# A second half of an out-projection taken four runs at a time for both token tiles, a weight unit released at the end of its first half, and small retention work moved to Pool

## Chip, cores and metric

The kernel runs on one core of a Trainium2 chip. The metric is device time in microseconds; the program is one launch. Three runs of the kernel before gave 1143.90, 1144.95 and 1144.04 us, median 1144.04 us.

## What is computed

A decoder of two layers over 256 tokens of width 1024, in float32. Cut to what matters:

```python
for layer in range(2):
    mixer = even_mixer if layer == 0 else odd_mixer      # MoBA (8 heads) + retention (4 heads) | 16 dilated heads
    h = h + mixer(rms_norm(h, mix_norm), w_in, w_out)    # ends in  concat(heads) @ w_out   (1024 x 1024)
    h = h + hier_moe(rms_norm(h, ffn_norm), ...)         # router: best of 4 groups, best 2 of its 8 experts
out = rms_norm(h, final_norm)

# retention: y = (scores * decay) @ v;  r_out = (y - mean) * rsqrt(var + eps) * silu(rg)
# expert:    y_e = (silu(x @ w_gate[e]) * (x @ w_up[e])) @ w_down[e]
```

With 256 tokens the mixers see two tiles of 128 tokens. Every one of the 32 experts of each layer is loaded and computed, with 32 slots an expert in a round.

## The kernel before

**Memory.** Weights stream through a ring of 12 units of 2 MB. In the expert loop units 0 to 7 hold four pairs (gate and up), units 8 to 11 four down matrices. Before the expert loop of a layer units 0 to 5 hold the input projection, units 6, 7, 8 and 11 activations, and `W_OUT_AT = (9, 10)` the two halves (512 output columns each) of the out-projection. `load_first` on SP issues the first four pairs and downs in a fixed order: pairs as the projection frees their units, then down 0 after the last values product, then downs 2 and 3 after the last product of the out-projection (`mixed` at 2T), then down 1, into unit 9, after the last logits. After that each load waits until the product that reads its unit is done (`next_pair`, `next_down`). SP's queue is in order.

**Precision.** The two projections are made of three fp32r products each: high by high, low by high, high by low. ACT makes the high part of a weight chunk (a copy to fp32r), DVE the low part (a subtraction). For the out-projection this is `split_mix` on ACT and `low_mix` on DVE, chunk by chunk in the order `MIX_TURNS`. A chunk is `(n, i)`: half n, run i of eight along the inner dimension. The low part overwrites the weight in place, the high part goes to one of three buffers of `mix_parts` (in `scratch`), to `mix_first` (four, in `xn`), or, for half 1 and i from 4 on, to `mix_last`, which lies in unit 9. `MIX_WAITS` holds how many uses of parts must be past before a buffer is written again.

**Out-projection (PE).** The first half is made for both tiles run by run (`mix_both`), in part between the last heads. Then PE's order is written out by hand: of the second half tile 0's runs 0 to 2, the turn (four transposes) of tile 0's first half, runs 3 and 4, the turn of tile 1's first half, runs 5 to 7; then tile 1's runs 0 and 1, turn, logits, runs 2 and 3, two blocks of logits, runs 4 to 7, and last tile 1's turn and logits. DVE adds each finished bank to h (`add_mixed`, L1589), ACT squares it for the norm and copies the turned parts to `hT`; tile 1's lie in unit 9.

**Routing.** `route` on DVE, once per tile, makes from the logits the best group, the best two experts and the one-hot sum `asg` (L1392 to L1416); PE sums places (L1199 to L1205) with a filler product (`keep_warm`, L879) between the two tiles; DVE makes the slot matrix (L1442); PE gathers the tokens (L990, 32 matmuls) and runs the first gate and up (L1008). Tile 0's normed rows are scaled on DVE (`scale_rows`, L1260), tile 1's on ACT (L834).

**Attention of layer 0.** PE makes scores (L938, L941) and transposes (L966), DVE mask and maximum (L1332), ACT the exponentials (L664), DVE reciprocals of the sums (L1345, L1346), Pool scales the probabilities (L622), ACT copies the turned ones (L672). Retention's group norm lies between the heads on DVE (`retention_step`): statistics, from Pool a power (L617), at m = 5 a Newton step of four operations (L1373 to L1376), at m = 6 and 7 the norm (L1382) and the product with the gate (L1385). The gate is made earlier by `swish`, in four pieces of 256 columns of three DVE operations each (L1284 add, L1285 reciprocal, L1286 product), two of them in the projection.

## Time and profile before

| what | value |
|---|---|
| three runs | 1143.90, 1144.95, 1144.04 us |
| profiled execution, its own time | 1143.11 us |
| its span | 1141.2 us |
| PE busy, share of the span | 863.9 us, 76% |
| DVE busy | 392.7 us, 34% |
| ACT busy | 239.8 us, 21% |
| POOL busy | 29.1 us, 3% |
| HBM read, mean rate | 439.01 MB, 386 GB/s |
| chain that ended last | PE 42%, DMA 39%, SPq 5%, DVE 5% |

The shares are averages over stages. The span falls into an input projection and attention of layer 0 (to about 103 us), its out-projection and routing (to 142), its expert loop (to 568), and the same for layer 1 (attention to 663, out-projection and routing to 701, experts to the end). In rows of the timeline a row is start, duration, engine, line, operation, operands and count, and in brackets the idle time before it and what ended it. Durations of neighbouring matmuls overlap, so their starts tell the pace.

### The profile page before, as it was taken

To read this page: it belongs to the slowest core of one execution; us is meant where nothing else is said; L and a number is where in the kernel's file an instruction comes from. 1 tells how busy PE (TensorE), PEld (TensorE's weight loads), DVE (VectorE), ACT (ScalarE), POOL (GpSimd) and SP (SyncE) were. 2 spreads that over 40 slices of the span, in tenths; PEclk is the share of its full clock that TensorE was granted. 3 is DMA by queue.
4 is the path that set the end of the run, shared out by engine and by line. 5 is a ranking of instruction groups with operands and counts; after the bars stand their busy time and mean duration, and the time that the engine had idled before them with its cause. 6 is when DMAs were issued, how large, how long until landed. Compare 5 with 4: busy or idle time off the path is not lost.

```text
span 1141.2 us, 21777 instructions
## 1 busy us (share of the span) xinstructions
PE 863.9 (76%) x9146; PEld 549.3 (48%) x9146; DVE 392.7 (34%) x988; ACT 239.8 (21%) x622; POOL 29.1 (3%) x47
## 2 busy tenths in 40 slices
PE   8999879976575757576799998798566666666774
PEld 6876745534243424243478776355243434343432
DVE  6887623322021212121188764233121212121212
ACT  5554401110010000000165762011000000000012
POOL 0002000000000000000000210000000000000000
PEclk9997979988787878788999998899787879797887
DMA  9866699999999999999997576999999999999995
GB/s 350 275 285 265 270 396 422 427 430 428 428 430 427 430 428 427 430 429 427 415 386 293 213 296 239 418 426 429 428 428 430 426 430 429 428 429 428 428 429 215
DMA packets 54417, 440.70 MB, mean 386 GB/s; under 512 B 11874, under 2 KB 12386, under 8 KB 29539
## 3 DMA queue, kind: packets, MB, share of 16 engines
q1 hardware_dynamic: 54368, 440.07, 92.9%
q8 instruction: 30, 0.49, 0.2%
q14 instruction: 17, 0.13, 0.0%
q10 hardware_dynamic: 2, 0.00, 0.0%
HBM read 439.01 MB, written 1.05 MB: 386 GB/s over the span
## 4 chain that ended last, share of the span: by engine, by line
PE 42%; DMA 39%; SPq 5%; DVE 5%; another core or an unknown queue 3%; ACT 3%; issue 2%; POOLq 0%; POOL 0%; ACTq 0%; DVEq 0%
DMA ring<-in_w_expert_up 21%; DMA ring<-in_w_expert_down 17%; PE bank L1008 12%; PE bank L1029 5%; PE bank L902 3%; PE bank L904 3%; PE bank L903 3%; PE bank L990 3%; SPq L441 3%; PE bank L1042 3%; PE bank L1090 1%; SPq L445 1%; PE bank L1092 1%; PE bank L1091 1%
## 5 line engine op out<-in xcount | busy, mean ns | idle before, releaser
L1008 PE MATMUL bank<-ring,scratch 128*32 128x256 f32 x4096 | 300.5, 458 | 176.9 <-DMA ring<-in_w_expert_up 175.5
L1008 PEld LDWEIGHTS bank<-ring,scratch 128*32 128x32 f32 x4096 | 155.1, 131 | 317.8 <-issue 207.0
L1471 DVE TENSOR_SCALAR scratch<-scratch 128x128 f32<-128x128 f32 x64 | 14.6, 227 | 632.2 <-ACT scratch L698 610.4
L697 ACT ACTIVATE scratch<-bank 128x128 f32<-128x128 f32 x64 | 17.8, 278 | 589.4 <-PE bank L1008 570.7
L1029 PE MATMUL bank<-ring,h 128*32 128x256 f32 x2048 | 127.4, 390 | 12.6 <-DMA ring<-in_w_expert_down 12.4
L1042 PE MATMUL bank<-h 32*128 32x256 f32 x1024 | 75.2, 407 | 37.2 <-ACT h L705 37.2
L1029 PEld LDWEIGHTS bank<-ring,h 128*32 128x32 f32 x2048 | 63.2, 111 | 57.3 <-issue 25.1
L1042 PEld LDWEIGHTS bank<-h 32*128 32x128 f32 x1024 | 50.6, 188 | 67.1 <-issue 67.0
L902 PE MATMUL bank<-split,h_high 128*128 128x512 f32 x192 | 77.2, 402 | 4.3 <-DVE split L1276 3.7
L904 PE MATMUL bank<-split,h_high 128*128 128x512 f32 x192 | 75.0, 391 | 0.0
L903 PE MATMUL bank<-split,h_low 128*128 128x512 f32 x192 | 74.9, 390 | 0.0
L1276 DVE SCALAR_TENSOR_TENSOR split<-ring,gains,split 128x512 fp32r<-128x512 f32 x96 | 67.9, 748 | 17.5 <-ACT split L744 16.8
L744 ACT ACTIVATE split<-ring,gains 128x512 fp32r<-128x512 f32 x96 | 65.5, 722 | 22.6 <-PE bank L904 20.9
L990 PE MATMUL bank<-scratch,xn 128*128 128x128 f32 x512 | 64.9, 288 | 1.7 <-DVE scratch L1442 1.7
L990 PEld LDWEIGHTS bank<-scratch,xn 128*128 128x128 f32 x512 | 61.9, 201 | 7.7 <-issue 7.7
L1472 DVE RECIPROCAL scratch<-scratch 128x128 f32<-128x128 f32 x64 | 61.0, 953 | 2.2
L705 ACT COPY h<-bank 128x256 f32<-128x256 f32 x64 | 23.8, 372 | 108.0 <-PE bank L1029 108.0
L1020 PE MATMUL bank<-cst,h 128*128 128x128 f32 x128 | 28.5, 305 | 21.5 <-DVE scratch L1459 11.0
L902 PEld LDWEIGHTS bank<-split,h_high 128*128 128x128 f32 x192 | 36.1, 188 | 14.1 <-DVE split L1276 6.7
L703 ACT COPY h<-bank 128x256 f32<-128x256 f32 x64 | 24.6, 385 | 72.4 <-PE bank L1020 72.2
L904 PEld LDWEIGHTS bank<-split,h_high 128*128 128x128 f32 x192 | 36.0, 188 | 7.9
L903 PEld LDWEIGHTS bank<-split,h_low 128*128 128x128 f32 x192 | 36.1, 188 | 6.9
(181 smaller groups left out, 742.8 us busy)
## 6 DMA issues: line engine op xcount, KB each, us to landing
ring<-in_w_expert_gate SPq DMA_DIRECT2D x64, 2048.0 KB, 47.3
ring<-in_w_expert_up SPq DMA_DIRECT2D x64, 2048.0 KB, 48.8
ring<-in_w_expert_down SPq DMA_DIRECT2D x62, 2048.0 KB, 48.4
ring<-in_w_in_even SPq DMA_DIRECT2D x5, 2048.0 KB, 17.5
ring<-in_w_in_odd SPq DMA_DIRECT2D x5, 2048.0 KB, 20.6
ring<-in_w_out_even SPq DMA_DIRECT2D x2, 2048.0 KB, 8.9
ring<-in_w_expert_down SPq DMA_DIRECT2D x4, 1024.0 KB, 44.6
ring<-in_w_out_odd SPq DMA_DIRECT2D x2, 2048.0 KB, 12.9
```

Of the source, the lines that this page charges most:

```text
L441: sp.dma_start(ring[:, unit, :], gate_rows[row]).then_inc(pair_arrived[l][k], 16)
L744: act.activation(w_high[u % PARTS], ring[:, j, 512 * c:512 * c + 512], ACT.Copy, scale=gains[:, 2 * l, c:c + 1]).then_inc(w_high_ready, 1)
L902: pe.matmul(bank, high, wh, start=(c == 0), stop=False)
L903: pe.matmul(bank, low, wh, start=False, stop=False)
L904: last = pe.matmul(bank, high, wl, start=False, stop=(c == C - 1))
L990: last = pe.matmul(psum[4 + c // 4][:, P * (c % 4):P * (c % 4) + P], xn_c[:, t, c, :], onehot[:, t, :, :].rearrange("p k s -> p (k s)"), s ...
L1008: last = pe.matmul(psum[6][32 * j:32 * j + 32, 0:2 * P].rearrange("p (a s) -> p a s", a=2), xT[:, c, SLOTS * k:SLOTS * k + SLOTS], ring[:, ...
L1020: last = pe.transpose(psum[7][:, P * t:P * t + P], gated[k][:, t, :, :].rearrange("p b s -> p (b s)"), ident)
L1029: last = pe.matmul(psum[4][32 * q:32 * q + 32, 0:QUARTER], hidT[k][:, 32 * j:32 * j + 32], ring[:, DOWN_AT[k], D * j + QUARTER * q:D * j + ...
L1042: last = pe.matmul(acc[q][:, t, :], gatedT[rows, P * t:P * t + P], y_sb[rows, :], start=False, stop=last_expert and t == T - 1, tile_posit ...
L1276: dve.scalar_tensor_tensor(out=w_low[u % PARTS], in0=ring[:, j, 512 * c:512 * c + 512], scalar=gains[:, 2 * l, c:c + 1], in1=w_high[u % PA ...
L1472: chain.link(dve.reciprocal(eb, eb))
```

## The change

Six things are altered. (1) PE's order in the second half of the out-projection: runs 4 to 7 for both tiles first, then the turns and the rest. (2) Where the high parts of the weights go: none lies in unit 9 any more, nor do tile 1's turned rows nor the squares' unused output; the counted waits follow. (3) SP loads down 1 after the first half (`mixed` at T). (4) Routing on DVE: tile 1's add before tile 0's routing, fewer operations, side results last; both tiles' rows are scaled on ACT. (5) Filler products on PE: two for one, and one of 256 columns before the gather. (6) On Pool: swish's add and product (512 columns at once), retention's Newton step, and the product of the normed rows with the gate; and one reciprocal for a head in place of two. Several semaphores of two layers become one, counted on.

```diff
-MIX_PART = (0, 1, 2, 3, 0, 1, 2, 0)
-MIX_WAITS = {(0, 4): 1, (0, 5): 2, (0, 6): 3, (0, 7): 5, (1, 3): 4}
-MIX_PARTS = 5
+MIX_PART = {(0, 0): 0, (0, 1): 1, (0, 2): 2, (0, 4): 0, (0, 5): 1, (0, 6): 2, (0, 7): 0,
+            (1, 4): 1, (1, 5): 2, (1, 6): 0, (1, 7): 1}
+MIX_WAITS = {(0, 4): 1, (0, 5): 2, (0, 6): 3, (0, 7): 5, (1, 3): 4, (1, 4): 6, (1, 5): 7, (1, 7): 8}
+MIX_PARTS = 8
+MIX_FIRST, MIX_LAST = (0, 4), (C - 1, 3)
-MIX_TURNS = (..., (0, 6), (1, 0), (0, 7), (1, 1), (1, 2), (1, 3), (1, 4), (1, 5), (1, 6), (1, 7))
+MIX_TURNS = (..., (0, 6), (1, 0), (0, 7), (1, 1), (1, 2), (1, 4), (1, 5), (1, 6), (1, 7), (1, 3))
...
@@ load_first (SP)
                 load_down(l, l * EXPERTS, 0)
+                sp.wait_ge(mixed, 2 * T * l + T)
+                load_down(l, l * EXPERTS + 1, 1)
                 sp.wait_ge(mixed, 2 * T * l + T * 2)
                 for k in range(2, GE):
                     load_down(l, l * EXPERTS + k, k)
-                sp.wait_ge(logits_done, T * (l + 1))
-                load_down(l, l * EXPERTS + 1, 1)
@@ gpsimd
+                if l == 0:
+                    for t in range(T):
+                        pool.wait_ge(bank_out[0][(RG * T + t) % 4], RG * T // 4 + 1)
+                        pool.tensor_tensor(rg[:, t, :], rg[:, t, :], const("ones")[:, 0:1].broadcast_to([P, 512]),
+                                           ALU.add).then_inc(swish_begun, 1)
+                        pool.wait_ge(swish_turned, T * (t + 1))
+                        pool.tensor_tensor(rg[:, t, :], rg[:, t, :], o_ret[:, t, :], ALU.mult).then_inc(swished, 1)
                 for m in range(HEADS[l]):
                     if l == 0 and m == 3:
                         pool.wait_ge(ret_var, 1)
+                        steps = ((rrstd, rvar, wide(half_exp[:, 0:1]), ALU.pow), (newton, rrstd, rrstd, ALU.mult),
+                                 (newton, newton, rvar, ALU.mult), (newton, newton, wide(half_exp[:, 0:1]), ALU.mult),
+                                 (newton, newton, wide(three_halves), ALU.add), (rrstd, rrstd, newton, ALU.mult))
+                        for n, (o, a, b, op) in enumerate(steps):
+                            pool.tensor_tensor(o, a, b, op).then_inc(ret_pow, 1)
+                            pool.wait_ge(ret_pow, n + 1)
...
+                    if l == 0 and m >= HEADS[0] - T:
+                        t = m - (HEADS[0] - T)
+                        pool.wait_ge(ret_scaled, t + 1)
+                        pool.wait_ge(swished, t + 1)
+                        pool.tensor_tensor(o_ret[:, t, :], o_ret[:, t, :], rg[:, t, :], ALU.mult).then_inc(ret_normed, 1)
@@ scalar
                 for t in range(T):
                     if t:
-                        act.wait_ge(rstd_ready, T * (2 * l + 1) + t + 1)
                         act.wait_ge(logits_done, T * l + t + 1)
-                        act.activation(xn_c[:, t, :, :], ...).then_inc(xn_scaled, 1)
+                    else:
+                        act.wait_ge(mix_xn_used, l + 1)
+                    act.wait_ge(rstd_ready, T * (2 * l + 1) + t + 1)
+                    act.activation(xn_c[:, t, :, :], h_c[:, t, :, :], ACT.Copy,
+                                   scale=rstd[:, t:t + 1]).then_inc(xn_scaled, 1)
+                for t in range(T):
                     act.wait_ge(gmax_ready, T * l + t + 1)
@@ tensor
-                mix_product(l, 1, 0, order[:3])
+                for i in order[4:]:
+                    for t in range(T):
+                        mix_product(l, 1, t, (i,))
                 turn_mixed(l, 0, 0)
-                mix_product(l, 1, 0, order[3:5])
+                mix_product(l, 1, 0, order[:2])
                 turn_mixed(l, 1, 0)
-                mix_product(l, 1, 0, order[5:])
+                mix_product(l, 1, 0, order[2:4])
                 pe.wait_ge(w_rt_ready, 1)
                 mix_product(l, 1, 1, order[:2])
                 turn_mixed(l, 0, 1)
                 logits(l, 0, 0)
                 mix_product(l, 1, 1, order[2:4])
                 logits(l, 0, 1)
+                turn_mixed(l, 1, 1)
                 logits(l, 1, 0)
-                mix_product(l, 1, 1, order[4:])
-                turn_mixed(l, 1, 1)
                 logits(l, 1, 1)
...
-                keep_warm(1, cst[:, 0:512], psum[0])
+                keep_warm(2, cst[:, 0:512], psum[0])
                 pe.wait_ge(assigned, T * l + 2)
...
-                pe.wait_ge(xn_ready, l + 1)
-                pe.wait_ge(xn_scaled, l + 1)
+                keep_warm(1, cst[:, 0:256], psum[0])
+                pe.wait_ge(xn_scaled, T * (l + 1))
@@ vector
-            def scale_rows(l, t):
...
             def swish(t, half, link):
-                link(dve.tensor_scalar(e, e, 1.0, None, ALU.add))
-                link(dve.reciprocal(e, e))
-                link(dve.tensor_tensor(e, e, gate_in, ALU.mult))
+                dve.wait_ge(swish_begun, t + 1)
+                dve.reciprocal(e, e).then_inc(swish_turned, 1)
...
-                dve.reciprocal(rden[:, m, 0:2], den[:, m, :])
-                dve.reciprocal(rden[:, m, 2:3], den[:, m, 1:2]).then_inc(den_ready[l], 1)
+                dve.reciprocal(rden[:, m % RDENS, :, :], den[:, m, :].unsqueeze(2).broadcast_to([P, T, 2])).then_inc(den_ready, 1)
...
                 elif m in (6, 7):
+                    if t == 0:
+                        dve.wait_ge(ret_pow, 6)
+                        dve.wait_ge(swished, T)
...
-                    dve.tensor_tensor(o_ret[:, t, :], o_ret[:, t, :], rg[:, t, :], ALU.mult).then_inc(ret_normed, 1)
...
                 if l == 0:
+                    swish(1, 0, link)
                     for n in range(2, RET):
                         decayed(n)
-                    swish(1, 0, link)
+                    swish(1, 1, link)
...
                 for t in range(T):
+                    low_mix(*late[t])
                     add_mixed(0, t)
-                    low_mix(*late[t])
...
-                for t in range(T):
-                    add_mixed(1, t)
-                    variance(2 * l + 1, t, 3 + t)
-                    inverse_root(2 * l + 1, t)
-                    if t == 0:
-                        scale_rows(l, t)
-                    route(l, t, route_link)
+                add_mixed(1, 0)
+                variance(2 * l + 1, 0, 3)
+                inverse_root(2 * l + 1, 0)
+                add_mixed(1, 1)
+                route(l, 0, route_link, lambda: variance(2 * l + 1, 1, 4))
+                inverse_root(2 * l + 1, 1)
+                route(l, 1, route_link)
```

In `route` the two casts of indices to float are gone (the comparisons read the integer indices), the penalty's factor is folded into one operation with the add, and the negated maximum and the difference of the best two (L1397, L1408) come after the one-hot sum.

## Rows read from the trace of the kernel before

**Rows 1.** Windows, core 0: length, busy us (x) of PE PEld DVE ACT POOL, clock, DMA, GB/s.

```profile
126.00:128.00 2.00, 2.00 (x17) 1.79 (x15) 0.68 (x3) 1.23 (x3) 0.41 (x1) 1.00 0.02 8
142.00:144.00 2.00, 1.99 (x9) 2.00 (x10) 0.85 (x6) 0.00 (x0) 1.12 (x4) 0.51 0.99 426
150.00:152.00 2.00, 1.28 (x25) 0.54 (x21) 0.00 (x0) 0.54 (x2) 0.00 (x0) 1.00 0.32 131
300.00:560.00 260.00, 172.59 (x2157) 98.55 (x2161) 50.43 (x117) 20.98 (x69) 0.00 (x0) 0.84 1.01 428
```

**Rows 2.** Waits of the DMA issuing queue: queue, line, releaser, total us, times, longest.

```profile
SPq L445 <- PE bank L1092: 40.7, 2, 20.4
```

**Rows 3.** Chain that ended last, layer 0, out-projection's end: start, us, work.

```profile
134.31 0.70 DVE h L1589
...
136.38 1.09 PE bank L1128 x8
142.01 5.43 PE bank L990 x32
147.44 3.63 PE bank L1008 x64
...
183.13 3.78 PE bank L990 x32
```

**Rows 4.** The same chain, layer 1.

```profile
694.63 1.62 PE bank L1128 x8
697.52 1.87 PE bank L879 x2
701.22 5.72 PE bank L990 x32
```

**Rows 5.** Timeline of PE, second half of the out-projection, layer 0.

```profile
119.11 0.39 PE L1090 MATMUL bank<-mix_first,o_high 128*128 128x512 f32 x1
...
129.57 0.98 PE L1128 MATMUL bank<-w_rt,scratch 128*128 128x36 f32 x8
...
131.27 0.48 PE L1090 MATMUL bank<-mix_last,o_high 128*128 128x512 f32 x1
...
133.88 0.39 PE L1092 MATMUL bank<-mix_low,o_high 128*128 128x512 f32 x1
...
137.97 1.10 PE L879 MATMUL bank<-cst 128*128 128x512 f32 x2
```

**Rows 6.** Timeline of DVE, routing of the second token tile, layer 0.

```profile
140.26 0.19 DVE L1416 TENSOR_TENSOR asg<-scratch 128x32 f32<-128x32 f32 x1
```

**Rows 7.** Timeline of ACT, the scaling of xn for tile 1, layer 0.

```profile
137.56 2.14 ACT L834 ACTIVATE xn<-h,small 128x1024 f32<-128x1024 f32 x1 [0.85 <-PE bank L1128]
```

**Rows 8.** Timeline of DVE, attention of layer 0.

```profile
93.99 0.75 DVE L1373 TENSOR_TENSOR small<-small 128x8 f32<-128x8 f32 x1
...
95.77 0.17 DVE L1376 TENSOR_TENSOR small<-small 128x8 f32<-128x8 f32 x1
```

**Rows 9.** Timeline of POOL, attention of layer 0.

```profile
92.28 1.65 POOL L617 TENSOR_TENSOR small<-small 128x8 f32<-128x8 f32 x1 [0.58 <-DVE small L1368]
93.89 1.61 POOL L622 TENSOR_TENSOR ring<-ring,small 128x384 f32<-128x384 f32 x2
```

**Rows 10.** Timeline of POOL, gate weights, layer 0.

```profile
142.62 0.20 POOL L605 TENSOR_TENSOR small<-small 128x2 f32<-128x2 f32 x1
```

**Rows 11.** Waits of PE in 84 to 104 us: line, releaser, total us, times, longest.

```profile
PE bank L938 <- DVE small L1332: 1.5, 2, 0.9
PE bank L966 <- ACT xn L672: 0.6, 1, 0.6
```

**Rows 12.** Timeline of PE, projection of layer 0, its one stall.

```profile
67.07 0.50 PE L902 MATMUL bank<-split,h_high 128*128 128x512 f32 x1 [0.89 <-DVE split L1276]
```

**Rows 13.** Chain that ended last, one head of layer 1.

```profile
656.25 0.14 DVE small L1346
```

More of the change, by code:

```diff
@@ L66 @@
 PROBS = 6
+RDENS = 12
 EXPERTS = 32
@@ L277, in build, with hT @@
         xT = scratch[:, 0:1024].rearrange("p (c s) -> p c s", c=C)
-        hT = [xT, ring[:, W_OUT_AT[0], 2048:2048 + D].rearrange("p (c s) -> p c s", c=C)]
+        hT_late = [v.rearrange("p (c s) -> p c s", c=C // 2) for v in (scratch[:, 1024:1536], xn[:, 1024:1536])]
+        def hT(t, q):
+            return hT_late[q] if t else xT[:, 4 * q:4 * q + 4, :]
         onehot = scratch[:, 1024:1280].rearrange("p (t k s) -> p t k s", t=T, k=GE)
@@ L303, in build @@
         top = small[:, 152:184].rearrange("p (a e) -> p a e", a=2 * T)
-        idx = small[:, 184:190]
         gv = small[:, 192:208]
@@ L314, in build @@
         cnt = small[:, 316:318]
+        three_halves = small[:, 318:319]
+        newton = small[:, 258:266]
         posm = sb("posm", [P, T, 36])
@@ L634, in square @@
                 if ph % 2:
-                    unused = mix_bank(1, t)[:, :] if half else ring[:, W_OUT_AT[0], 3072 + 512 * t:3584 + 512 * t]
+                    unused = mix_bank(1, t)[:, :] if half else psum[4 + t][:, :]
                 else:
@@ L665, in exponentials @@
                                           accum_out=den[:, m, t:t + 1])
-                last.then_inc(exp_done[l], 1)
+                last.then_inc(exp_done, 1)
             def copy_pT(l, m):
@@ L687, in split_mix @@
                     act.wait_ge(pair_done[l], HEADS[l] // 2)
-                if n and i == C // 2:
+                if (n, i) == (1, 6):
                     act.wait_ge(mixed, 2 * T * l + T)
@@ L878, in keep_warm @@
                 for _ in range(n):
-                    pe.matmul(bank[:, :], data[:, 0:P], data, start=True, stop=True)
+                    pe.matmul(bank[:, 0:data.shape[1]], data[:, 0:P], data, start=True, stop=True)
             def turn_part(ph, t, q):
@@ L1089, in mix_product @@
                     out = mix_bank(n, t)[:, :]
-                    pe.matmul(out, high, mix_high(n, i), start=(i == 0), stop=False)
+                    pe.matmul(out, high, mix_high(n, i), start=(i == MIX_FIRST[n]), stop=False)
                     pe.matmul(out, low, mix_high(n, i), start=False, stop=False)
-                    last = pe.matmul(out, high, mix_low[n][:, c, :], start=False, stop=(i == C - 1))
-                    if (n, t) == (0, 1) and i < MIX_PARTS:
+                    last = pe.matmul(out, high, mix_low[n][:, c, :], start=False, stop=(i == MIX_LAST[n]))
+                    if t and (i < C - 1 if n == 0 else i == MIX_FIRST[1]):
                         last.then_inc(mix_part_used, 1)
@@ L1127, in logits @@
                 for c in range(4 * q, 4 * q + 4):
-                    last = pe.matmul(psum[4 + t][:, 0:36], hT[t][:, c, :],
+                    last = pe.matmul(psum[4 + t][:, 0:36], hT(t, q)[:, c - 4 * q, :],
                                      w_rt[:, l, c, :], start=(c == 0), stop=(c == C - 1))
@@ L1383, in retention_step, with route @@
                                                  rstat[:, t, n, 0:1], rrstd[:, at:at + 1], ALU.subtract, ALU.mult)
-                    link(last)
-                    dve.tensor_tensor(o_ret[:, t, :], o_ret[:, t, :], rg[:, t, :], ALU.mult).then_inc(ret_normed, 1)
-            def route(l, t, link):
+                    last.then_inc(ret_scaled, 1)
+            def route(l, t, link, between=None):
                 dve.wait_ge(logits_done, T * l + t + 1)
@@ L1406, in route @@
                 best = top[:, T + t, :]
                 link(dve.max(best, masked[:, t, :]))
+                if between:
+                    between()
+                link(dve.max_index(idx_u[:, T + t, :], best, masked[:, t, :]))
+                link(dve.tensor_tensor(chosen[:, t, :, :],
+                                       const("iota")[:, 0:EXPERTS].unsqueeze(1).broadcast_to([P, 2, EXPERTS]),
+                                       idx_u[:, T + t, 0:2].unsqueeze(2).broadcast_to([P, 2, EXPERTS]), ALU.is_equal))
@@ L1408, in route @@
+                dve.tensor_tensor(asg[:, t, :], chosen[:, t, 0, :], chosen[:, t, 1, :], ALU.add)\
+                   .then_inc(assigned, 1)
+                dve.tensor_scalar(gv[:, t:t + 1], top[:, t, 0:1], -1.0, None, ALU.mult)
                 dve.tensor_tensor(gv[:, 6 + t:7 + t], best[:, 1:2], best[:, 0:1], ALU.subtract)\
                    .then_inc(gmax_ready, 1)
-                link(dve.max_index(idx_u[:, T + t, :], best, masked[:, t, :]))
-                pair = idx[:, 2 + 2 * t:4 + 2 * t]
@@ L1555, in _ @@
                         head_max(l, m)
-                    if l == 0 and m == 1:
-                        swish(1, 1, link)
                     if l == 0 and m == HEADS[l] + 2:
```

89 lines of the change are left out of this document (35 added, 54 removed).

## The prediction

> **What bounds the kernel now.** First the windows. From 300 to 560 us, inside the first layer's expert loop, the DMA engines are busy for the whole stretch (share 1.01) and move 428 GB/s [rows 1]: there the time is bytes over rate, and no engine's speed counts. In front of each expert loop it is different. At 126 to 128 us the share is 0.02, because the ring is full or the next unit is not yet given up, and at 150 to 152 us it is 0.32 [rows 1]. The issuing queue stood up to 20.4 us before the loads of the second half's weight units, for the out-projection's last product [rows 2]. But those loads are done by about 150.6 us, and the next one can be issued only when the first expert's gate-up matmuls, which begin at 147.44 and last 3.63 us, have given up their pair [rows 3]: 151.1 us. So the end of that first gate-up decides, once per layer: all later bytes of the layer follow it, and each us that it comes earlier is a us of the kernel. Third, the chain: in front of it lie the residual add at 134.31, the last logits at 136.38, the gather at 142.01, the gate-up at 147.44 [rows 3], and in layer 1 the same steps [rows 4].
>
> **The tail of the out-projection, reordered.** One product is three matmuls; the last four run from 131.27 to 134.1, where the matmul of 133.88 hands over [rows 5], so one takes some 0.7 us, or 0.68 with the handover at its start taken off. The second half has 16 of them and begins at 119.11. Before, two blocks of logits (129.57 to 131.27, 1.70 us [rows 5]) and the first tile's products stand ahead of the last four products, which end at 133.88 + 0.39 = 134.3. After, eight products for both tiles come first, then three turns of some 0.4 us, four products for each tile and one block of logits between: the last product ends at 119.1 + 16 x 0.68 + 1.2 + 0.8 + 0.2 = 132.3, about 2.0 us earlier. The price is that tile 0 is complete only at 128.2. Its norm takes some 3 us, to 131.5, and its logits end at 133.2, which is when DVE turns to its routing. So tile 0's routing, which was hidden under tile 1's products, now runs while tile 1's last logits are made, and DVE becomes the one that is late: routing 0 from 133.2, with tile 1's variance between, to 136.2, two short steps of the root to 136.8, routing 1 to its one-hot sum at 139.1. That sum stood at 140.26 + 0.19 = 140.45 [rows 6], so of the 2.0 us 1.35 arrive. Counted in this is that the two casts go (an estimate of 0.2 us each, from the 0.19 us of the small operation beside them [rows 6]) and that the two side results move behind the sum. The scaling of xn goes to ACT for both tiles, 2.14 us each (137.56 [rows 7]): it begins after the last turned copy, at 134.5, and ends near 139.0, and DVE's scaling goes. It stays under the routing, 1.6 us before the gather; if that cover went it would cost what it overruns. The new parts buffers wait on products that are at least 1 us past when their copy is due, so I cost these waits at nothing. SP's load for expert 1 moves from behind the logits to the end of the first half: that empties the queue earlier, but the first gate-up's end still decides, so 0.
>
> **The clock.** The gather of 32 matmuls takes 3.78 us at full clock (183.13 [rows 3]), but 5.43 at 142.01 [rows 3] and 5.72 at 701.22 [rows 4]; the granted clock is 0.51 at 142 to 144 us [rows 1], that is 1.2 GHz, after a stretch in which PE had only turns, logits and waits. The change puts two filler products of 512 columns where one was, and a short one just before the gather. Three outcomes, counted from the second half's start. (a) The rate never falls: gather from 140.65 to 144.4, against 147.44: 3.0 us saved; layer 1, whose part runs at half rate from the logits on (1.62 against 1.09 us), saves 4.3: 7.3 together. (b) It falls in the thin stretch, which has grown longer, since the products that stood behind the logits now stand before them. The fillers then hold PE: one took 1.10 us at full [rows 5] and 1.87 at half [rows 4], so two are 3.7, and they end 2.2 us after the sum that they were to bridge; but the rate is back for the gather: 0.6 and 1.8 saved, 2.4 together. (c) It falls later and the gather is slow as well: 1.2 lost together. I take 2.9, near (b) with a part of (a), because already the shorter stretch of before lost the rate in layer 1.
>
> **Attention of layer 0.** DVE is the bound at its start: scores wait 1.5 us in two waits for DVE's masks, and a transpose 0.6 us for a copy that is late for the same reason [rows 11]. The change takes from DVE the swish adds and products, the Newton steps (one of them takes 0.75 us [rows 8]) and the two 512-column products. The matmuls run at half rate in that stretch and are nearly gapless from 92 us, so no more than those 2.1 us can be won, and not less than 0: I take 1.1 (0.5 at the start, 0.6 at the copy). Pool's part: its power of 8 columns takes 1.65 us [rows 9], a product of 2 columns 0.20 [rows 10]; the five steps are products and sums, so 0.28 us each with the wait (an estimate): 1.4 us, behind which the fourth head's scaling queues. It is then ready at 95.9, and PE wants it at 96.7. The last two products of 512 columns (1.07 us each, from 0.80 for 384 [rows 9]) end near 101.4, and PE wants them at 104.
>
> **Projection of layer 0.** PE has one stall, 0.89 us, behind the swish on DVE [rows 12]. Without its adds and products 0.3 us of it would go. But the two engines get in each other's way: a DVE product of 8 columns with two operands from SBUF took 0.75 us while Pool worked (93.99 [rows 8] inside 93.89 to 95.50 [rows 9]) and 0.17 after (95.77 [rows 8]). Pool's four passes of 1.07 us now lie among the splits of the weights, which are such operations. With no collision 0.3 is won; with every pass in the way 4.3 - 0.3 = 4.0 is lost. I take 0.6 lost, two passes of which half is covered by the four split buffers. The Trainium skill (GPSIMD Engine Reference, Key points) says that Pool shares its SBUF interfaces with VectorE and collides with operations of two SBUF inputs, and that elementwise work is about twice as fast on DVE; by that rule alone the move to Pool gains nothing. The trace agrees on the collision.
>
> **Layer 1's attention.** One reciprocal in place of two for each head: the second one is 0.14 us in the chain [rows 13], some 0.09 after overlap, in about 6 of 16 heads: 0.5 us.
>
> **Sum**, against the profiled execution (1143.11 us, span 1141.2): -2.9 - 1.1 + 0.6 - 0.5 = -3.9, so 1139.2. The three runs shown (1143.9 to 1144.95) are 0.8 to 1.8 above that execution, whose gathers were not at their slowest; I keep 1139.2 for the after kernel's median, since its tail price is a middle one already.
>
> **Rivals.** R1: the first gate-up's end is not what decides, the transfers are: then nothing moves, 1143.1. For it: 428 GB/s for most of the time. Against it: share 0.32 and 0.02 just in front [rows 1]. It also stands for gains eaten up by collisions of 2 to 4 us. R2: outcome (a) in both layers, 1143.1 - 7.3 - 1.0 = 1134.8. For it: the filler is doubled. Against it: the thin stretch grows. R3, slower: Pool's Newton steps cost as its power of the same width does, 1.65 us [rows 9] and not 0.28. Five of them hold the fourth head until 103, against PE's 97.0 of before; PE, in order, loses 5.9 us in place of winning 1.1, and the sum is 1143.1 + 5.9 - 2.4 - 0.5 + 0.1 = 1146.2, with the tail as in (b) and 0.1 lost in the projection. It decides above 0.45 us a step. Against it: 0.20 for two columns [rows 10]. R4: the change doesn't do as it says: a late buffer (the last parts copy waits on a product of the same half) stalls PE inside the eight products; each us of that takes one us of the tail, so up to the 1.35 in each layer: 1141.9.
>
> **How the numbers follow.** Forecast 0.60, R1 0.13, R2 0.12, R3 0.06, R4 0.09. A measurement of this kernel tells 0.2 per cent, 2.3 us, from no change, so the bounds are 1141.8 and 1146.3. Faster: forecast's part below 1141.8 (0.54), R2 0.12, half of R4 and a part of R1: 0.76. Slower: half of R3 and twice-failed cases, 0.06. Same: 0.18. Extremes of the terms are 1132 (all best) and 1146.5; the range leaves out R3 and half of R2: 1135.3 to 1143.4.
>
> **What would show it.** Right: last product of the second half 13.2 us after its start in both layers, the sum of the second routing 1.3 us earlier, gathers at 3.8 us, the first gate-up's end 2 to 4 us earlier in each layer after taking off what attention gave, DMA share near 1 from there. In layer 0 the mix begins 0.5 us earlier, DVE's splits of 0.75 us are longer beside Pool. Wrong: the DMA share below 1 behind the first gate-up; PE stalls inside the eight products; Pool's steps above 0.45 us; fillers at 1.9 us and a slow gather together.

## The result, and the profile after

Four runs of the changed kernel gave 1134.06 to 1136.33 us, median 1135.59; four of the kernel before, interleaved with them, 1143.90 to 1146.07, median 1144.49. The ratio is 0.9919, interval 0.9903 to 0.9935: 8.9 us faster. The forecast was 1139.2, from 1135.3 to 1143.4: the sign was right, the time lies just inside the low end of the range, and the gain is more than twice the 3.9 us of the sum. The profiled execution took 1135.6 us (span 1133.7), 7.5 us less than the one of before.

Page of the changed kernel: busy time, rates, and the chain's shares.

```profile
PE 861.8 (76%) x9154; PEld 547.3 (48%) x9154; DVE 383.3 (34%) x940; ACT 244.2 (22%) x624; POOL 37.8 (3%) x59
HBM read 439.01 MB, written 1.05 MB: 388 GB/s over the span
PE 43%; DMA 40%; SPq 5%; DVE 4%; another core or an unknown queue 3%; ACT 3%; issue 2%; POOL 0%; POOLq 0%; ACTq 0%; DVEq 0%
```

PE's work is the same. DVE has 9.4 us less, Pool 8.7 us more, and neither number is near the 7.5 us or has to be: what counts is when each layer's first gate-up ends. Windows of the changed kernel, columns as in [rows 1]:

```profile
126.00:128.00 2.00, 2.00 (x15) 1.72 (x13) 1.00 (x3) 0.91 (x3) 0.10 (x1) 1.00 0.88 377
142.00:144.00 2.00, 2.00 (x32) 1.45 (x35) 0.69 (x1) 0.00 (x0) 0.00 (x0) 1.00 0.02 8
300.00:560.00 260.00, 172.29 (x2164) 98.60 (x2168) 49.75 (x116) 21.41 (x71) 0.00 (x0) 0.84 1.01 428
```

The expert loop is what it was (share 1.01, 428 GB/s). The DMA engines now work at 126 us, where they stood at 0.02, because the load into unit 9 goes out after the first half; and they stand still at 142 to 144, until the gate-up is done. The chain of the changed kernel, out-projection's end to gate-up, layer 0 (start, us, work):

```profile
134.36 3.22 PE bank L910 x4
137.58 0.27 PE bank L1236 x2
...
139.07 3.81 PE bank L1021 x32
142.88 3.63 PE bank L1039 x64
```

and layer 1:

```profile
694.44 0.41 PE bank L1236 x2
...
695.94 3.81 PE bank L1021 x32
699.75 3.63 PE bank L1039 x64
```

Beside [rows 3] and [rows 4]: the gather takes 3.81 us in both layers, where it took 5.43 and 5.72, and the gate-up begins 4.6 us earlier in layer 0 and some 7.2 us earlier in layer 1 (699.75 against 706.94).

The span splits into these stages, from the timelines (us). Each runs from the first matmul of one kind to the first of the next; attention begins with the last projection product. Before and after are one profile each:

| stage | before | after | gain |
|---|---|---|---|
| start, to the first projection product | 9.77 | 10.65 | -0.9 |
| projection, layer 0 | 72.56 | 72.11 | 0.45 |
| attention, layer 0, to the first out-projection product | 20.77 | 18.63 | 2.1 |
| out-projection, first half, layer 0 | 16.01 | 15.33 | 0.7 |
| **tail, layer 0**: second half's first product to first gate-up | 28.26 | 26.10 | 2.2 |
| expert loop, layer 0 | 425.85 | 427.49 | -1.6 |
| projection, layer 1 | 70.31 | 70.31 | 0 |
| attention, layer 1 | 20.03 | 20.26 | -0.2 |
| out-projection, first half, layer 1 | 13.79 | 13.79 | 0 |
| **tail, layer 1** | 29.52 | 25.01 | 4.5 |
| the rest | 434.32 | 434.07 | 0.25 |

The start and the expert loops vary by about 1 us between kernels that don't differ there (9.1 to 10.7, and 425.9 to 427.5 in the profiles below), so the two losses are nothing to explain. The two tails are 6.7 us, attention and the first half 2.8. The name "second sum" below is for the one-hot sum of tile 1's routing, the last step of DVE that PE's place sums wait for.

### The profile page after: what moved, and what is told of

It is laid out like the page before. It is cut to its first block, busy times and chain, and to the rows that moved or that the text cites. A ratio compares the mean times of both kernels' runs of the same rounds, so it can differ in the third digit from the quotient of the medians.

```text
span 1133.7 us, 21763 instructions
## 1 busy us (share of the span) xinstructions
PE 861.8 (76%) x9154; PEld 547.3 (48%) x9154; DVE 383.3 (34%) x940; ACT 244.2 (22%) x624; POOL 37.8 (3%) x59
## 4 chain that ended last, share of the span: by engine, by line
PE 43%; DMA 40%; SPq 5%; DVE 4%; another core or an unknown queue 3%; ACT 3%; issue 2%; POOL 0%; POOLq 0%; ACTq 0%; DVEq 0%
DMA ring<-in_w_expert_up 30%; PE bank L1039 13%; DMA ring<-in_w_expert_down 9%; PE bank L1060 5%; PE bank L933 3%; PE bank L935 3%; PE bank L934 3%; SPq L449 3%; PE bank L1073 3%; PE bank L1021 2%; PE bank L1121 1%; SPq L453 1%; PE bank L1123 1%; PE bank L1122 1%
## 5 line engine op out<-in xcount | busy, mean ns | idle before, releaser
L1060 PEld LDWEIGHTS bank<-ring,h 128*32 128x32 f32 x2048 | 63.1, 111 | 55.8 <-issue 24.1
L772 ACT ACTIVATE split<-ring,gains 128x512 fp32r<-128x512 f32 x96 | 65.5, 722 | 21.7 <-PE bank L935 20.3
L1021 PE MATMUL bank<-scratch,xn 128*128 128x128 f32 x512 | 61.4, 278 | 0.7 <-DVE scratch L1459 0.7
L1021 PEld LDWEIGHTS bank<-scratch,xn 128*128 128x128 f32 x512 | 58.4, 192 | 7.2 <-issue 7.2
```

The lines of the kernel that those rows point to most:

```text
L772: act.activation(w_high[u % PARTS], ring[:, j, 512 * c:512 * c + 512], ACT.Copy, scale=gains[:, 2 * l, c:c + 1]).then_inc(w_high_ready, 1)
L1021: last = pe.matmul(psum[4 + c // 4][:, P * (c % 4):P * (c % 4) + P], xn_c[:, t, c, :], onehot[:, t, :, :].rearrange("p k s -> p (k s)"), s ...
L1060: last = pe.matmul(psum[4][32 * q:32 * q + 32, 0:QUARTER], hidT[k][:, 32 * j:32 * j + 32], ring[:, DOWN_AT[k], D * j + QUARTER * q:D * j + ...
```

## Experiments

Twelve kernels were run, each timed in five rounds beside the kernel before (1143.86, 1144.78 and 1144.2 us median in the three groups of four). Lengths named "tail" are those of the table.

| kernel | median us | ratio to before, interval | tail 0 | tail 1 |
|---|---|---|---|---|
| the changed kernel again | 1135.39 | 0.9920 (0.9905 to 0.9936) | 26.1 | 26.1 |
| Pool's moves undone | 1137.52 | 0.9945 (0.9930 to 0.9960) | 25.0 | 26.1 |
| one filler | 1139.72 | 0.9960 (0.9944 to 0.9976) | 26.6 | 27.8 |
| kernel before with the fillers | 1142.82 | 0.9985 (0.9975 to 0.9995) | 26.6 | 27.5 |
| down 1 loaded late | 1137.83 | 0.9934 (0.9917 to 0.9952) | 25.0 | 25.0 |
| tile 1's add late | 1145.53 | 1.0008 (0.9999 to 1.0017) | 31.8 | 31.2 |
| two reciprocals | 1134.14 | 0.9909 (0.9895 to 0.9923) | 25.0 | 27.2 |
| Newton step on DVE | 1134.90 | 0.9915 (0.9900 to 0.9930) | 25.8 | 25.9 |
| swish and gate products on DVE | 1135.41 | 0.9928 (0.9913 to 0.9944) | 25.0 | 25.0 |
| tile 1's add late, one filler | 1146.30 | 1.0026 (1.0016 to 1.0035) | 30.8 | 32.1 |
| long fillers of 384 columns | 1134.45 | 0.9918 (0.9903 to 0.9933) | 25.0 | 25.0 |
| one more short filler | **1133.63** | 0.9914 (0.9900 to 0.9928) | 25.0 | 25.0 |

**The changed kernel again**, unaltered, for the spread.

> The changed kernel once more, to see how its gain falls on the stages when the clock's falls lie elsewhere. Every theory: 1134 to 1137 us. Order theory (the reordered products and the shorter routing bring the one-hot sum earlier): the second routing's sum ends 19.7 us after the second half's start in both layers, as in the profile seen, against 21.3 and 21.9 before. Clock theory (most of the tail's gain is that the gather runs at full rate): the gather takes 3.8 us in both layers again, and in neither layer the way from second half to first gate-up is longer than 27 us (28.3 and 29.5 before).

1135.39 us, the same. The second sum ended 19.7 us after the second half's start in both layers, and the gather took 3.81 us in both, as either theory had it. Its layer 1 tail was 26.1 where the first profile had 25.0, so a tail alone varies by 1.1 us; the next section comes back to it.

**All of Pool's new work back on DVE**, the merged reciprocal kept.

```diff
-                        pool.tensor_tensor(rg[:, t, :], rg[:, t, :], o_ret[:, t, :], ALU.mult).then_inc(swished, 1)
...
+                link(dve.tensor_scalar(e, e, 1.0, None, ALU.add))
+                link(dve.reciprocal(e, e))
+                link(dve.tensor_tensor(e, e, gate_in, ALU.mult))
...
-                        for n, (o, a, b, op) in enumerate(steps):
+                    link(dve.tensor_tensor(step, rrstd, rrstd, ALU.mult))
...
-                        pool.tensor_tensor(o_ret[:, t, :], o_ret[:, t, :], rg[:, t, :], ALU.mult).then_inc(ret_normed, 1)
+                    dve.tensor_tensor(o_ret[:, t, :], o_ret[:, t, :], rg[:, t, :], ALU.mult).then_inc(ret_normed, 1)
```

> The changed kernel with swish, Newton step and the gate's product back on DVE. If the move to Pool is what made attention of layer 0 shorter (20.8 us before, 18.6 after from last projection product to first mix product), it takes 20.5 to 21 us again and the kernel is 2 to 3 us slower than the changed one, 1137.6 to 1138.6. Rival: attention is shorter because the clock fell 2.8 us later in it; then it stays at 18.6 to 19.3 and the kernel is within 0.5 us of the changed one.

1137.52, between the two expectations, so the moves are worth 2.1 us. The projection is 72.55 (72.11 with the moves) and attention 19.79 (18.63): 1.6 of them lie there, and PE's time at half rate in attention was 6.8 us in both profiles. The waits of PE in its attention of layer 0 (line, releaser, total, times, longest), first here and then in the changed kernel:

```profile
PE bank L951 <- DVE small L1340: 2.2, 3, 0.9
PE bank L979 <- ACT xn L682: 1.1, 1, 1.1
```

```profile
PE bank L969 <- DVE small L1356: 2.0, 3, 0.7
PE bank L997 <- ACT xn L700: 0.4, 1, 0.4
```

The moves shorten one wait for a late copy (1.1 to 0.4) and hardly the waits for masks. The kernel before had 1.5 and 0.6 [rows 11], no more than the changed kernel's 2.0 and 0.4: from before to after, PE's waits in this stretch did not shrink.

**One filler**: the changed kernel with the filler products of before.

```diff
-                keep_warm(2, cst[:, 0:512], psum[0])
+                keep_warm(1, cst[:, 0:512], psum[0])
...
-                keep_warm(1, cst[:, 0:256], psum[0])
```

> The changed kernel with one filler product of 512 columns, as before, and without the short one. Clock theory: the gather runs at half rate in at least one layer (5.4 us and more), the kernel is 2 to 4 us slower than the changed one, 1137.6 to 1139.6. Order theory: the fillers only fill; within 0.7 us of the changed one, and where the rate has fallen PE reaches the second routing's sum up to 1 us earlier.

1139.72: 4.3 us slower than with them, as the clock theory had it. Timeline of PE in this kernel, layer 0:

```profile
134.15 1.10 PE L910 MATMUL bank<-cst 128*128 128x512 f32 x2
136.43 0.41 PE L1236 MATMUL bank<-asg,cst 128*128 128x32 f32 x2 [1.18 <-DVE asg L1429]
...
137.93 5.44 PE L1021 MATMUL bank<-scratch,xn 128*128 128x128 f32 x32 [0.87 <-DVE scratch L1458]
```

PE idles 1.18 us behind its filler and 0.87 before the gather, the granted clock is 0.63 at 138 to 140 us, and the gather takes 5.44 us (6.25 in layer 1).

**The kernel before with the fillers**, nothing else changed but that a filler writes only as many columns as it reads.

```diff
-                keep_warm(1, cst[:, 0:512], psum[0])
+                keep_warm(2, cst[:, 0:512], psum[0])
...
+                keep_warm(1, cst[:, 0:256], psum[0])
                 pe.wait_ge(xn_ready, l + 1)
```

> The kernel before with two filler products of 512 columns and the short one, nothing else. Clock theory: most of the tail's 6.6 us of gain come from them, 3 to 5 us faster than before, 1139.5 to 1141.5. Order theory: the stretch from last product to second sum is long enough already and the gather's rate differs by chance; 0 to 1.5 us faster, 1143 to 1144.5.

1142.82, 1.0 us faster in the median (1.7 by the ratio), although its tails are 1.6 and 2.0 us shorter in the profile. The gather ran at full rate in both layers, 3.81 us, as the clock theory had it, but the 3 to 5 us that it gave did not come. Its projection was 1.25 us longer in the profile, 73.81: the granted clock was 0.50 from 12 to 15 us, among the first projection products. The kernel with two reciprocals (73.4) has the same, and in the one with the Newton step on DVE (73.0) matmuls ran at half pace up to 13.8 us. So, in one profile each, fillers alone shorten the two tails by 3.7 us, the new order and routing alone (the kernel with one filler) by 3.4, and both together by 5.6 to 7.8; in the median, fillers alone are worth 1.0 to 1.7 us.

**Down 1 loaded late**, behind the last logits as before.

```diff
-                sp.wait_ge(mixed, 2 * T * l + T)
-                load_down(l, l * EXPERTS + 1, 1)
...
+                sp.wait_ge(logits_done, T * (l + 1))
+                load_down(l, l * EXPERTS + 1, 1)
```

> The changed kernel with expert 1's down matrix loaded after the last logits again, as before. Theory that the first gate-up's end decides: nothing, within 0.7 us of the changed kernel; the three loads begun at the last product are done 12.9 + 14.7 us after the second half's start, 1.6 us behind the first gate-up's start and before its end. Rival, the transfers decide now that the gate-up comes earlier: 1 to 4 us slower than the changed kernel.

1137.83, 6.9 us under its kernel before where the changed kernel has 8.5: 1.5 us less gain, though the intervals overlap. Both tails are 25.0, so it is not PE. A window of this kernel, and the same one of the changed kernel:

```profile
700.00:705.00 5.00, 4.28 (x80) 2.35 (x76) 0.00 (x0) 0.54 (x2) 0.00 (x0) 1.00 0.92 354
```

```profile
700.00:705.00 5.00, 4.28 (x84) 2.34 (x80) 0.47 (x1) 0.54 (x2) 0.00 (x0) 1.00 0.22 49
```

The next pair was issued at 702.6 here, but the DMA engines were still busy with the downs (0.92 against 0.22): the pair stands behind them. The rest of layer 1 took 436.6 us, against 433.4 to 434.9 in all other profiles. In layer 0 the expert loop took 427.0, inside the spread of the others, so the loss shows in one layer alone.

**Tile 1's add and variance behind tile 0's routing**, as DVE had them before.

```diff
                 inverse_root(2 * l + 1, 0)
-                add_mixed(1, 1)
-                route(l, 0, route_link, lambda: variance(2 * l + 1, 1, 4))
+                route(l, 0, route_link)
+                add_mixed(1, 1)
+                variance(2 * l + 1, 1, 4)
```

> The changed kernel with tile 1's add and variance behind tile 0's routing, as before. The add would come 2.3 us after its product instead of at once, and with it the last turn and logits: second sum at about 22 us after the second half's start instead of 19.7, kernel 2 to 4 us slower than the changed one. Rival, clock: the fillers hide it, since after a fall PE is late anyway; under 1 us slower.

1145.53: 0.75 us above its kernel before, where the changed kernel is 8.5 below: a loss of 9 us, far above what either theory expected. Its timeline of PE, layer 0:

```profile
133.69 1.00 PE L916 MATMUL bank<-cst,h 128*128 128x128 f32 x4 [3.19 <-DVE h L1605]
...
139.03 3.76 PE L910 MATMUL bank<-cst 128*128 128x512 f32 x4
142.58 0.47 PE L1236 MATMUL bank<-asg,cst 128*128 128x32 f32 x2
```

and of DVE:

```profile
140.15 0.19 DVE L1430 TENSOR_TENSOR asg<-scratch 128x32 f32<-128x32 f32 x1
```

Tile 1's last product was done at 129.7, but DVE routed tile 0 until 132.9, so PE stood 3.19 us. In the kernel before the two fell together: there the last product ended at 134.3 and the routing sum had been done since 133.5. The turn and the logits behind the wait then ran at half rate (the granted clock was low from 133.9 for 10.2 us), and so did the fillers, 3.76 us, so that PE came to the sum, ready at 140.34, only at 142.58. Tail 31.8 against 26.1: 4.3 of the 5.7 us lie in the second sum, which comes 24.0 us after the second half's start and not 19.7, and 1.3 in the fillers.

**The same with one filler.**

> The changed kernel with tile 1's add and variance behind tile 0's routing, and with the one filler of the kernel before in place of two and a short one: the new order of products with both other helpers of the tail taken away. With the fillers there, the late add cost 10 us (1145.5), 4.3 us a tail of it in the second sum and the rest in fillers that ran at half rate and ended 2.4 us behind that sum. Theory A (the add is what the new order needs, the fillers only add to its price): the second sum stays at 24.0 us after the second half's start, PE is free when it comes, but the gather is at half rate: tails of 31.0 to 32, median within 1.5 us of 1145.5. Theory B (the 10 us are mostly the fillers'): tails of 28.5 to 29.5 us as in the kernel before, median 1140 to 1142.

1146.3, tails 30.8 and 32.1: as the theory that the add is the cause had it, but for layer 0's second sum, which came at 23.0 us and not 24.0 (24.1 in layer 1). Layer 0:

```profile
137.61 2.06 PE L910 MATMUL bank<-cst 128*128 128x512 f32 x2
139.46 0.47 PE L1236 MATMUL bank<-asg,cst 128*128 128x32 f32 x2
...
141.22 5.55 PE L1021 MATMUL bank<-scratch,xn 128*128 128x128 f32 x32 [0.87 <-DVE scratch L1458]
```

What the shorter filler gives back (0.5 us behind the sum in place of 2.2), the gather takes (5.55 for 3.81). The change without the early add and the fillers is 2.1 us slower than the kernel before.

**Two reciprocals per head.**

```diff
-                dve.reciprocal(rden[:, m % RDENS, :, :], den[:, m, :].unsqueeze(2).broadcast_to([P, T, 2])).then_inc(den_ready, 1)
+                for t in range(T):
+                    last = dve.reciprocal(rden[:, m % RDENS, t, :], den[:, m, t:t + 1].broadcast_to([P, 2]))
+                last.then_inc(den_ready, 1)
```

> The changed kernel with two reciprocals for each head again. My forecast's term: 0.5 us slower, all in layer 1's attention (20.3 us to 20.8 from last projection product to first mix product). Rival, the profile seen: layer 1's attention took 20.03 us before and 20.26 and 20.27 after, so the single reciprocal brings nothing; within 0.3 us in that stretch.

1134.14, not slower: layer 1's attention is 20.04 us with two reciprocals, and 19.9 to 20.3 in the profiles with one. No gain of the merged operation can be told.

**Newton step back on DVE.**

> The changed kernel with the Newton step alone back on DVE. Attention of layer 0 took 18.6 us in the changed kernel and 19.8 with all of the small work back on DVE. If the Newton step makes that difference (its products collide with Pool's scaling, 0.75 us each), 19.6 to 20.2 and 1 to 1.5 us slower; if the swish and gate products make it, 18.6 to 18.9 and within 0.4 us.

1134.90, no difference that can be told. Attention took 19.34 us, which fits neither expectation, but PE ran at half rate for 10.2 us of it and not for 6.8 (next section). On Pool the step was six operations in 3.05 us:

```profile
92.41 3.05 POOL L639 TENSOR_TENSOR small<-small 128x8 f32<-128x8 f32 x6 [0.58 <-DVE small L1391]
```

so 1.4 us more than the power alone [rows 9], 0.28 a step. By the time, it does not matter which engine does it.

**Swish's adds and products and the gate products back on DVE**, the Newton step left on Pool.

> The changed kernel with the gate's adds and products (swish) and the product of the normed rows with the gate back on DVE; retention's Newton step stays on Pool. Theory A (these large operations, and not the Newton step, are what attention and the projection's stall gained): projection 72.5 us (72.1 in the changed kernel), last projection product to first out-projection product 19.8 us (18.6), median 1.5 to 2.2 us above the changed kernel's, as with all moves to Pool undone (1137.5). Theory B (the Newton step carries half of it): 19.2 us, median at most 1 us higher.

1135.41, ratio 0.9928: between the two theories. The projection is 72.60. The 0.89 us stall of [rows 12] stands in all four profiles with swish on DVE and in none of the ten with it on Pool, so the 0.5 us there are these operations'. Attention is 19.54, and it was 19.34 with the Newton step back; kernels with every move had 19.3 to 19.6 where the low stretch of the clock was as long as in these two, 10.2 us (next section). So each group alone costs attention nothing there. Both together cost 1.1 us, but that pair of profiles had a low stretch of 6.8 us; no profile has both moves undone at 10.2 us, or one of them at 6.8. Whether the moves pay only together, or only where the low stretch is short, stays open.

**Long fillers of 384 columns.**

```diff
-                keep_warm(2, cst[:, 0:512], psum[0])
+                keep_warm(2, cst[:, 0:384], psum[0])
```

> The changed kernel with the two long fillers of 384 columns in place of 512. Theory A (fillers at half rate hold PE beyond the sum): they take 2.8 us in place of 3.7 at half rate, so they end with the sum or 0.3 us behind it; a tail in which the rate falls costs 25.3 in place of 26.1 us, and the gather still runs at full rate (3.8 us); median 0.4 to 0.8 us lower. Theory B (it is the fillers' length that brings the rate back before the gather): the gather falls to half rate in one layer or both, 5.2 to 5.7 us in place of 3.8, tails of 26.6 to 27.8, and the median 1 to 4 us higher, as with one filler.

1134.45. The rate did not fall in either tail, so the case that separates the theories did not come up. With 2 x 384 columns and the short filler the gather took 3.81 us in both layers of this one profile; what these fillers cost at half rate is not shown.

**One more short filler**, where PE's stretch is thin.

```diff
                 logits(l, 0, 1)
+                keep_warm(1, cst[:, 0:256], psum[3])
                 turn_mixed(l, 1, 1)
```

> The changed kernel with one more short filler (256 columns) on PE between the last logits of tile 0 and the turn of tile 1. Theory A (the granted rate falls in the thin stretch of turns and 36-column matmuls, and the two long fillers at half rate then end about 1.1 us after the sum they bridge; this happened in about half of the tails looked at so far): the rate holds in both layers, both tails (second half's start to first gate-up) are 25.0 us plus at most 0.3, and the median is 0.5 to 1.2 us below the changed kernel's, about 1134.6. Theory B (whether the rate falls there hangs on what lies further back, so that a filler at this place changes nothing): tails of 25.0 to 26.6 as before, median equal or up to 0.8 us higher, since the filler itself holds the last logits by 0.4 us.

1133.63, the lowest median of all, 10.6 us under its kernel before (by the ratio, two reciprocals are as low). Its five runs lie within 1.6 us (1133.3 to 1134.85) where six of the changed kernel span 3.9. Timeline of PE in this kernel, layer 0:

```profile
131.17 0.68 PE L910 MATMUL bank<-cst 128*128 128x256 f32 x2
131.69 0.60 PE L916 MATMUL bank<-cst,h 128*128 128x128 f32 x4
...
134.67 1.96 PE L910 MATMUL bank<-cst 128*128 128x512 f32 x4
136.95 0.41 PE L1237 MATMUL bank<-asg,cst 128*128 128x32 f32 x2 [0.32 <-DVE asg L1431]
...
138.45 3.81 PE L1021 MATMUL bank<-scratch,xn 128*128 128x128 f32 x32 [0.35 <-DVE scratch L1460]
```

The short filler costs nothing, since DVE takes up tile 1's logits later than they are ready; the long ones take 1.96 us and PE waits for the sum and not the reverse. That it is better than the changed kernel, by 0.7 us (ratios) to 1.8 (medians), is not shown: the intervals of the ratios overlap, and three other kernels had both tails at 25.0 without it.

## Why the prediction was right in sign and wrong in size

**The bound.** Right: the end of the first gate-up decides. What moved the medians by more than 2 us were edits that moved the two tails or layer 0's attention. R1 did not occur, but is closer than the forecast had it: it said that SP's earlier load of down 1 is worth 0. With the tail as short as it is now, the kernel without that load had its transfers behind the first gate-up in layer 1, and lost some 1.5 us (intervals overlap).

**The tail's mechanism.** Right where it was worked out. The last matmul of the products starts 12.95 us after the second half's start (14.77 before) and hands over at 13.2, as forecast, though the forecast's own terms add up to 132.2 and not 132.3. The second sum ends at 19.71 (forecast 20.0, before 21.34). Of these 1.63 us, 1.04 are that DVE takes up tile 1's logits earlier (17.42 after the start, before 18.46), and 0.59 that it needs 2.29 us to the sum and not 2.88, by the operations that went and those that come later. No late buffer stalls PE (R4 is out). What the forecast passes over is the condition for all of it: it names tile 1's variance between the steps of routing 0, but not tile 1's add ahead of them. With both where they were, the whole gain of 9 us is gone.

**The clock: the step that failed.** The term that was mis-sized is the 2.9 us for the two tails. The forecast weighed three outcomes, and took that much because it held the fall of the rate in the thin stretch, outcome (b), for much the likeliest: "the fillers then hold PE [...] they end 2.2 us after the sum that they were to bridge; but the rate is back for the gather: 0.6 and 1.8 saved, 2.4 together." Measured: 2.2 and 4.5 in the profile, 2.2 and 3.4 in its repeat. Of outcome (a), 3.0 and 4.3, layer 1 is a case; layer 0 lies between (a) and (b). Over the seven kernels that have this tail unaltered (the changed kernel twice, Pool's moves, down 1, reciprocals, Newton, swish) the fourteen tails are seven times 25.0, six times 25.8 to 26.1, and once 27.2; their mean is 25.6, so two tails cost 51.2 us against 57.8 in the one profile of before. Two things were mis-sized. The first is how often the rate falls: it held in half of the tails, where the forecast had argued from the length of the thin stretch. That stretch did grow longer, but it also grew denser. In the 4 us after the last product PE is busy for 3.78 us in both layers (130 to 134 and 687.9 to 691.9), where it was for 2.54 (134.2 to 138.2 and 692.4 to 696.4). The kernel before had these waits behind its last product, for the add and for the copy:

```profile
135.05 0.66 PE L885 MATMUL bank<-cst,h 128*128 128x128 f32 x4 [0.78 <-DVE h L1589]
...
136.38 1.08 PE L1128 MATMUL bank<-w_rt,ring 128*128 128x36 f32 x8 [0.68 <-ACT ring L817]
```

In the changed kernel a block of tile 0's logits stands in the first of them, and a block of tile 1's in the second. That the denser stretch is why the rate held is not shown: both layers have the 3.78 us, and in layer 0 the rate fell. The second is what a fall costs. In six of the seven it came late. The changed kernel's timeline of PE, layer 0:

```profile
134.19 3.38 PE L910 MATMUL bank<-cst 128*128 128x512 f32 x4
137.37 0.47 PE L1236 MATMUL bank<-asg,cst 128*128 128x32 f32 x2
```

and layer 1, where it did not fall:

```profile
692.16 1.96 PE L910 MATMUL bank<-cst 128*128 128x512 f32 x4
694.44 0.41 PE L1236 MATMUL bank<-asg,cst 128*128 128x32 f32 x2 [0.32 <-DVE asg L1430]
```

The low stretch lasted 3.4 us, from 134.6; the logits were past, the fillers took 3.38 us in place of 1.96, and PE came to its next product 0.95 us behind the sum (136.42), not 2.2. So such a fall makes the tail 26.1 and costs 1.1 us, where (a) and (b) of the forecast lie 2.4 us apart. Outcome (b) itself is real, and came once in the fourteen, in layer 1 of the kernel with two reciprocals, whose second sum was done at 693.92:

```profile
692.31 3.76 PE L910 MATMUL bank<-cst 128*128 128x512 f32 x4
...
695.86 0.47 PE L1236 MATMUL bank<-asg,cst 128*128 128x32 f32 x2
```

There PE is 1.9 us behind the sum, the gather takes 3.83, and the tail is 27.2. The kernel with the late add shows the same, 2.2 us behind. The term is short by 2.7 to 3.8 us; what the whole forecast lacked is 3.6. What makes the rate fall in one execution and hold in the next stays open.

**Attention of layer 0.** Forecast 1.1, measured 2.1, and 0.7 more in the first half behind it. Undoing the moves gives 1.1 back, so the size of the term is right. But PE's waits, from which it was taken, came to 2.1 us before and 2.4 after. What was left out is again the rate. Windows of 82 to 104 us, before and then after:

```profile
82.00:104.00 22.00, 19.87 (x98) 12.80 (x97) 19.94 (x87) 11.64 (x41) 8.16 (x9) 0.70 0.73 286
```

```profile
82.00:104.00 22.00, 19.61 (x114) 13.58 (x113) 14.42 (x70) 12.17 (x43) 12.84 (x17) 0.84 0.73 286
```

The granted clock is 0.84 in place of 0.70: PE was at half rate for 6.8 us from 93.6 in place of 13.7 from 90.8. Of the twelve profiles in the new order four have the 6.8 us and eight 10.2 us; with all of Pool's moves attention is 18.6 us in the first case and 19.3 to 19.6 in the second. So 3.4 us more at half rate cost some 0.8 here, and the forecast held this stretch to be slow in any case. In the kernel before, half rate also reached 1.4 us into the first half, to 104.5, where the changed kernel was back at 100.5; that fits the 0.7. What makes the stretch 6.8 or 10.2 us long was not found.

**Projection.** Forecast 0.6 lost, measured 0.45 won. The stall of [rows 12] went whole, not by a third: in the changed kernel PE runs through there. The collisions exist, but cost little. Pool's passes of 512 columns, an add of a constant and a product of two full rows:

```profile
60.72 1.04 POOL L626 TENSOR_TENSOR ring<-ring,cst 128x512 f32<-128x512 f32 x1 [42.34 <-ACT ring L783]
66.52 1.64 POOL L629 TENSOR_TENSOR ring<-ring 128x512 f32<-128x512 f32 x1 [4.76 <-DVE ring L1310]
```

The add took 1.04 us with DVE idle and 1.48 beside DVE's splits. The product took 1.64 beside a split and 1.27 in its three places in attention. And DVE's splits of the weights, in the projection of the changed kernel and then of the one before (busy, mean ns):

```profile
L1302 DVE SCALAR_TENSOR_TENSOR split<-ring,gains,split 128x512 fp32r<-128x512 f32 x48 | 35.5, 782 | 7.2 <-ACT split L772 6.7
```

```profile
L1276 DVE SCALAR_TENSOR_TENSOR split<-ring,gains,split 128x512 fp32r<-128x512 f32 x48 | 34.0, 748 | 8.8 <-ACT split L744 8.4
```

1.5 us more in 48 of them, against 7.2 us that DVE idles among them, nearly all for ACT's part: the collisions fit into DVE's slack. The Trainium skill (GPSIMD Engine Reference, Key points) says that Pool shares its SBUF interfaces with VectorE, and the trace agrees, by the 0.75 us against 0.17 of [rows 8]. It also puts elementwise work at about twice as fast on DVE, and again the trace agrees: the product of 512 columns took 0.69 us on DVE in the kernel before and 1.27 on Pool. That did not decide this case: the moves gave 2.1 us.

**Layer 1's reciprocal.** Forecast 0.5, measured nothing. **R3** is out: 0.28 us a step, as estimated, and the kernel is no slower for it.

**The sum by its terms**, forecast and then profile: tails 2.9 and 6.7; attention with the first half behind it 1.1 and 2.8; projection -0.6 and 0.45; reciprocal 0.5 and -0.2. The two terms in which the clock's rate stands were short by 3.8 and 1.7 us, the projection by 1.0; the reciprocal took 0.7 back, and the start and the expert loops took 2.3, by chance: without that luck of the draw the profiled gain would have been 9.8 us and the forecast further off.

## What to carry over

Count, in each profile, for how long the tensor engine ran at half rate and which work stood in it, and give that its own cases in the sum: here 1.1 us behind a filler, 1.6 in a gather and 0.8 in attention were each as large as any operation that was moved. A reordering of one engine's work can hang on the order of the engine that serves it: look for the one operation that the new order makes urgent (here an add of 0.69 us, worth 9 us). When a stage in front of a transfer-bound loop gets shorter, look anew at loads that were free to be late.

## What was not expected of the hardware

- The same kernel shows tails of 25.0 and 26.1 us in different executions, with the granted clock low for a part of it or not; nothing that was varied here says which it will be. With one more short filler both were 25.0 in its one profile, but so they were in three kernels without it.
- PE that stands 3.19 us and then makes only turns and 36-column logits was at half rate for the next 10.2 us (the late add); in the kernel with a filler of 0.5 us before the same turn and logits the clock stayed at 1.00 through both tails.
- Chains of operations on 8 columns cost 0.28 us each on Pool, wait included, where its power of the same width takes 1.65.
